# One attention-values product per head, by blocks of keys, in place of two query halves in two slots

## The reference

```
for i in range(S // Q_BLOCK):                       # 4 blocks of 128 queries
    lo, hi = i * Q_BLOCK, (i + 1) * Q_BLOCK
    s = einsum('bhqd,bhkd->bhqk', q[lo:hi], k[:hi]) * scale + cum[lo:hi] - cum[:hi]
    s = where(kpos <= qpos, s, -1e30)
    prob = softmax(s)
    outs.append(einsum('bhqk,bhkd->bhqd', prob, v[:, :, :hi]))   # values
```

## Time and profile before

| | us |
|---|---|
| median of 3 runs (lowest to highest) | 1625.31 (1624.86 to 1625.37) |
| the profiled execution | 1624.74 |
| its span | 1623.0 |
| PE busy in the span | 1604.3 |
| DVE busy | 1027.8 |
| ACT busy | 696.0 |

### The profile page before, as it was taken

The page is one execution under the profiler, slowest core; times in us unless marked ns, Lnnn a source line. Parts: engine busy times, 40 slices in busy tenths (PEclk is TensorE's granted clock), DMA queues, the critical chain, the costliest instruction groups (busy, mean ns, idle before and its releaser), DMA issues.

```text
span 1623.0 us, 19202 instructions
## 1 busy us (share of the span) xinstructions
PE 1604.3 (99%) x7616; PEld 1326.4 (82%) x7616; DVE 1027.8 (63%) x1455; ACT 696.0 (43%) x1016; POOL 174.4 (11%) x255
## 2 busy tenths in 40 slices
PE   9999999999999999999999999999999999999998
PEld 7878777888888888887788887888888888888888
DVE  6755788668384865657744578445567636736757
ACT  6524475545252524414662155342344314414544
POOL 0001145100000000024500255000000000000000
PEclk9999999999999999999999999999999999999999
DMA  5223231265757532331122211323322222222331
GB/s 189 81 89 138 87 128 53 77 209 130 234 130 233 130 104 88 121 130 54 51 104 78 100 56 53 137 97 104 104 91 104 104 92 90 104 104 83 120 109 52
DMA packets 30584, 176.17 MB, mean 109 GB/s; under 512 B 4064, under 2 KB 6560, under 8 KB 11040
## 3 DMA queue, kind: packets, MB, share of 16 engines
q1 hardware_dynamic: 24048, 151.81, 26.0%
q0 software_dynamic: 1728, 12.58, 4.0%
q10 hardware_dynamic: 4720, 10.56, 1.8%
HBM read 170.72 MB, written 4.23 MB: 108 GB/s over the span
## 4 chain that ended last, share of the span: by engine, by line
PE 89%; DVE 5%; issue 2%; ACT 2%; POOL 1%; DMA 1%; SPq 0%; DVEq 0%; POOLq 0%
PE bank L719 22%; PE bank L721 21%; PE bank L720 21%; PE bank L727 3%; PE bank L729 3%; PE bank L728 3%; PE bank L1107 2%; PE bank L1108 2%; PE bank L1109 2%; PE bank L920 1%; PE bank L905 1%; PE bank L1025 1%; DMA x<-in_x_t 1%; DVE q_blk L1991 0%; DVE k_blk L1991 0%
## 5 line engine op out<-in xcount | busy, mean ns | idle before, releaser
L719 PE MATMUL bank<-a_hi,w_hi 128*128 128x512 f32 x1184 | 465.5, 393 | 1.6 <-DVE w_lo L2073 0.9
L721 PE MATMUL bank<-a_hi,w_lo 128*128 128x512 f32 x1184 | 461.2, 390 | 0.0
L720 PE MATMUL bank<-a_lo,w_hi 128*128 128x512 f32 x1184 | 460.9, 389 | 0.0
L1291 ACT ACTIVATE w_hi<-w_raw 128x2048 fp32r<-128x2048 f32 x105 | 200.3, 1908 | 219.0 <-DMA w_raw<-in_strips 215.6
L1854 DVE TENSOR_TENSOR w_lo<-w_raw,w_hi 128x2048 fp32r<-128x2048 f32 x102 | 233.7, 2292 | 48.0 <-ACT w_hi L1291 47.9
L719 PEld LDWEIGHTS bank<-a_hi,w_hi 128*128 128x128 f32 x1184 | 222.4, 188 | 47.5 <-issue 1.4
L721 PEld LDWEIGHTS bank<-a_hi,w_lo 128*128 128x128 f32 x1184 | 222.2, 188 | 46.9
L720 PEld LDWEIGHTS bank<-a_lo,w_hi 128*128 128x128 f32 x1184 | 222.4, 188 | 44.0 <-issue 0.2
L719 PE MATMUL bank<-b_hi,w_hi 128*128 128x512 f32 x368 | 143.4, 390 | 0.4 <-DVE b_lo L2570 0.4
L720 PE MATMUL bank<-b_lo,w_hi 128*128 128x512 f32 x368 | 143.2, 389 | 0.0
L721 PE MATMUL bank<-b_hi,w_lo 128*128 128x512 f32 x368 | 143.2, 389 | 0.0
(11 more groups left out here) (362 smaller groups left out, 2570.3 us busy)
## 6 DMA issues: line engine op xcount, KB each, us to landing
w_raw<-in_strips SPq DMA_DIRECT2D x117, 1024.0 KB, 4.8
a_part<-in_parts SPq DMA_DIRECT2D x15, 1024.0 KB, 7.0
a_part<-in_parts POOLq DMA_DIRECT2D x12, 1024.0 KB, 9.9
seg_in<-cum_kept ACTq DMA_DIRECT2D x16, 256.0 KB, 3.5
spare<-in_parts SPq DMA_DIRECT2D x3, 1024.0 KB, 14.7
spare<-in_strips SPq DMA_DIRECT2D x3, 1024.0 KB, 4.7
x<-in_x_t SPq DMA_DIRECT2D x4, 512.0 KB, 6.8
head_bias<-in_rel ACTq DMA_DIRECT2D x1, 2048.0 KB, 10.5
```

The costliest lines, as they stand in the source:

```text
L719: mm(ps[:, :], w_hi[slot][:, k, cols], hi[:, k, :], start=(k == 0), stop=False)
L720: mm(ps[:, :], w_hi[slot][:, k, cols], lo[:, k, :], start=False, stop=False)
L721: return mm(ps[:, :], w_lo[slot][:, k, cols], hi[:, k, :], start=False, stop=(k == kt - 1))
L1291: run(w_hi[j], w_raw[j], ACT.Copy).then_inc(hi_split, 1)
```

## The change

All values of a head are computed at one place, slot m = 4 head + 7. There they stand ahead of the slot's dense pieces, behind scores(n), where values(head, 1) stood behind turn(n - 2). They go by blocks of keys: for key block 0 one matmul pair (pt_hi, pt_lo) over all four query blocks, for key block 1 a pair over query block 1 and a pair over blocks 2 and 3, for key block 2 a pair over blocks 2 and 3, for key block 3 a pair over block 3. pv_done counts once a head instead of twice, and every wait on it is rewritten: the keep of a head's tiles waits for all values of the head before, where the keep of its tiles 0 and 1 waited for the first half alone.

```diff
+KEY_BLOCKS = [(0, 0, 4, 0), (1, 8, 9, 1), (1, 4, 6, 2), (2, 6, 8, 2), (3, 9, 10, 3)]
...
-                    sp_eng.wait_ge(pv_done, 2 * 3 * HEADS8)
+                    sp_eng.wait_ge(pv_done, 3 * HEADS8)
...
-                def values(head, second):
-
-                    pe.wait_ge(p_lo_done, t0 + TT * head + 2 * second + 2)
-                    if head >= 2 and not second:
+                def values(head):
+
+                    pe.wait_ge(p_lo_done, t0 + TT * (head + 1))
+                    if head >= 2:
                         pe.wait_ge(att_out, h0 + head - 1)
-                    for j in range(2 * second + 2):
-                        alone = j == 2 * second + 1
-                        blocks = BLOCKS[2 * second + 1]
-                        at = range(10)[blocks][j]
-                        cols = slice(at, at + 1) if alone else slice(at - 1, at + 1)
-                        dst = bank[6 + head % 2][:, 256 * second + P * alone:256 * second + 256]
+                    for j, first, end, i in KEY_BLOCKS:
+                        dst = bank[6 + head % 2][:, i * P:(i + end - first) * P]
                         for part in (pt_hi, pt_lo):
...
                 for n in range(SLOTS[call]):
                     if n < TILES and n and (lead is None or n >= 2):
                         scores(n)
+                    if n - late >= 7 and (n - late) % TT == 3:
+                        values((n - late - 7) // TT)
                     for p in slot_pieces(n, call):
                         dense(p)
...
                         turn(n - late - 2)
-                    if n - late >= 5 and (n - late) % 4 == 1 and n - late < TILES + 4:
-                        values((n - late - 5) // TT, 0)
-                    if n - late >= 7 and (n - late) % 4 == 3:
-                        values((n - late - 7) // TT, 1)
...
-                        act.wait_ge(pv_done, 2 * (h0 + head - 1) + i // 2 + 1)
+                        act.wait_ge(pv_done, h0 + head)
...
-                    act.wait_ge(pv_done, 2 * (h0 + head + 1))
+                    act.wait_ge(pv_done, h0 + head + 1)
```

More of the change, by code:

```diff
@@ L906, in turn @@
                     last.then_inc(turned, 1)
-                def values(head, second):
-                    pe.wait_ge(p_lo_done, t0 + TT * head + 2 * second + 2)
-                    if head >= 2 and not second:
+                def values(head):
+                    pe.wait_ge(p_lo_done, t0 + TT * (head + 1))
+                    if head >= 2:
                         pe.wait_ge(att_out, h0 + head - 1)
-                    for j in range(2 * second + 2):
-                        alone = j == 2 * second + 1
-                        blocks = BLOCKS[2 * second + 1]
-                        at = range(10)[blocks][j]
-                        cols = slice(at, at + 1) if alone else slice(at - 1, at + 1)
-                        dst = bank[6 + head % 2][:, 256 * second + P * alone:256 * second + 256]
+                    for j, first, end, i in KEY_BLOCKS:
+                        dst = bank[6 + head % 2][:, i * P:(i + end - first) * P]
                         for part in (pt_hi, pt_lo):
                             last = mm(dst, vs[:, j, head, :, :].rearrange("p s f -> p (s f)"),
-                                      part[:, cols, :].rearrange("p b q -> p (b q)"), start=(j == 0 and part is pt_hi),
+                                      part[:, first:end, :].rearrange("p b q -> p (b q)"), start=(j == 0 and part is pt_hi),
                                       stop=(j > 0 or part is pt_lo), skip_group_check=(j > 0))
```

## The result

| | before | changed |
|---|---|---|
| median us (lowest to highest, 5 runs each) | 1624.95 (1624.86 to 1625.37) | 1650.62 (1645.61 to 1652.04) |
| the profiled execution, its span | 1624.74, 1623.0 | 1645.61, 1643.9 |

The ratio of the times is 1.015, 95% interval 1.0138 to 1.0161. The change makes the kernel slower by some 26 us. The forecast was 1642, the range 1629 to 1652. The profiled execution of the changed kernel is its fastest; the other four are slower than it by up to 6.4 us, where the five of the kernel before lie within 0.5. So there are two questions: where the 20.9 us between the two traces come from, and where the rest comes from.

What follows compares the result with a forecast made beforehand. A once-per-head loop through PE, DVE and ACT was taken to bound the attention calls. 13.6 us for 2a and 2b plus 3.1 for call 1 gave 16.7 more, 1642; own range 1631 to 1650, 8-in-10 range 1629 to 1652.

Steps and rivals of the forecast that it cites:

- E: In each attention head, the end of DVE's low part of the head's last tile, for which PE waits.
- The loop E, PE, scores, DVE and ACT, next E: Once per head in the attention calls: matmuls put between E and the next scores lengthen it; PE's part was 1.56 us.
- Fewer matmuls: Values of each head: 10 matmuls for 12, 1.45 us becoming 1.36, at most 2.2 us of PE's work over 24 heads.
- the 0.96: Us by which scores in a 2a or 2b head were forecast to end later after E: E + 2.52 against E + 1.56.
- The values stand ahead of the dense piece: At the values' new place PE waits 2.06 us for E, and the scores end 0.96 us later.
- The keep of the next head's first tile: ACT's keep waits for all values; the wait grows some 0.5 us but adds nothing beyond the scores' delay.
- The rival of whole waits: PE's extra waits come through whole, 1.5 x 21 heads, 31.5 us more, 1657; chance 0.07.
- the tails: Behind head 6 of 2a and 2b, with no scores left, PE is the bound: 1.5 us later per call.
- The end of call 1: Last values ahead of three dense pieces, so the next product's 0.7 us wait for its fourth operand tile goes away.
- The clock: Rival: idle times of about 2 us per head halve the clock in one stretch, 70 us more, 1712; chance 0.02.

Runs made afterwards that it cites:

- e2: The kernel before with only the second half of the values moved ahead of the slot's dense pieces, still two halves; 1636.98 us, ratio 1.0073.
- e4: The kernel before with the second half of the values one slot later, behind the next scores; 1623.15 us, ratio 0.9987.
- e8: The changed kernel with an extra pv_done count behind key block 0's pair, for which the keep of a head's first tile waits; 1647.97 us, ratio 1.014.
- e1: Against the kernel before, all values of a head in one run, but behind the slot's transposes where the second half stood; 1642.28 us, ratio 1.0108.
- a0_again: The changed kernel run once more, unaltered, for its scatter; 1650.85 us (1647.30 to 1651.43), ratio 1.0153 against the kernel before.
- e9: The kernel with all values in one run behind the transposes, plus an early pv_done count behind key block 0's pair; 1633.60 us, ratio 1.005.
- e6: The changed kernel with four matmuls that compute nothing ahead of the values' wait in all heads; 1649.76 us.
- e7: The changed kernel with four matmuls that compute nothing ahead of the values' wait, only in heads 0 to 6 of 2a and 2b; 1647.12 us, ratio 1.0138.

## Why the prediction was right, and where not

*What bounds the kernel.* The loop E, PE, scores, DVE and ACT, next E is shown: E-to-scores grew by 1.12 us in the head of the timeline and the loop by 1.12; the stretch behind the scores kept its length; e2 put 0.7 into it and e4 took the values out, with the signs the loop gives.

*Fewer matmuls.* 1.36 us for the ten were forecast. Where PE doesn't wait they take 1.34, as PE's timeline of the changed kernel in call 1 shows:

```profile
249.79 0.40 PE L918 MATMUL bank<-pt_hi,vs 128*128 128x512 f32 x1
250.03 0.40 PE L918 MATMUL bank<-pt_lo,vs 128*128 128x512 f32 x1
...
251.13 0.45 PE L721 MATMUL bank<-y_hi,w_hi 128*128 128x512 f32 x1
```

In the head above they take 1.43 (1012.68 - 1011.25), since the first one behind a wait steps 0.34 (1011.59 - 1011.25) for 0.24 here (250.03 - 249.79). Only two of the 24 heads have the 1.34; the others have 1.42 to 1.45, and before the two halves of nearly every head took 0.49 and 0.96, 1.45 together. So the waiting takes back nearly all that the merging was to give. Together with the dense piece behind the values (0.75 for 0.69, its first matmul stepping 0.29 for 0.23) this is most of the 0.16 by which the 1.12 exceeds the 0.96.

*The values stand ahead of the dense piece.* Right: e2 alone gives +11.7. The wait at the values is 1.48 us in the head where I had 2.06, and only 0.87 or 0.88 in eight of the twelve loops of 2a and 2b, for 1.5 to 2 forecast: PE reaches the values later than I had put it. The length of the loop doesn't hang on that, since PE waits for E either way.

*The keep of the next head's first tile.* This is the step that was wrong in part. "Lies inside the delay already counted" holds in the middle heads of the changed kernel (e8 leaves their loops at 9.2 us). It fails in the first heads of 2a and 2b; in that of 2a DVE has a weight split behind that low part. DVE there, in the changed kernel (E = 766.60), and below it the split and the maximum in the kernel before (E = 762.05):

```profile
768.67 0.29 DVE L2009 TENSOR_TENSOR pt_lo_2a<-bank,pt_hi_2a 128x128 fp32r<-128x128 f32 x1 [1.63 <-ACT pt_hi_2a L1347]
768.88 1.52 DVE L1865 TENSOR_TENSOR w_lo<-w_raw,w_hi 128x1024 fp32r<-128x1024 f32 x1
770.33 0.41 DVE L1999 CUSTOM_DVE_ANT_0 score_2a<-bank,future 128x256 f32<-128x256 f32 x1
...
762.70 1.25 DVE L1869 TENSOR_TENSOR w_lo<-w_raw,w_hi 128x1024 fp32r<-128x1024 f32 x1
763.86 0.41 DVE L2003 CUSTOM_DVE_ANT_0 score_2a<-bank,future 128x256 f32<-128x256 f32 x1
```

The maximum comes at E + 3.73 (in the first head of 2b at E + 3.41), not at the E + 2.9 of the other heads: 1.63 us of idling, and then 1.5 us of work that before ran while PE was on its way to the scores. The rival of whole waits had named this as its condition, that PE delays the others twice in a head. Outside the new place the semaphore is no detail: it is 8.7 of the 17.0 us of e1.

*Sizes.* Between the traces, from the first scores of call 1 to those of 2a 4.6 us were added (forecast 3.1), from there to those of 2b 8.5 (6.8), and in the rest 7.8 (6.8): 20.9 for 16.7. The six loops of 2a are 6.7 us longer together and those of 2b 5.7, for 5.3 forecast, single ones between 0.65 and 1.83; the tails, from head 6's E to head 7's, are 1.4 and 1.7 longer, for 1.5. In call 1 the sum hides luck: six loops at 0.47 were forecast, and they grew by 0.26, 0.01, 0.01, 0.81, 0.03 and 1.42, which is 2.5 for 2.8. The lower end of the forecast's own range was mis-added as well: 1625.3 and half of the delay, 8 us, is 1633 and not 1631.

*The end of call 1.* Wrong sign: the wait for b_lo grew from 0.7 to 1.4 us. No run tried it, but the traces show the path. DVE before, then ACT and DVE now:

```profile
307.64 0.69 DVE L2223 TENSOR_TENSOR x<-x,bank 128x512 f32<-128x512 f32 x1 [3.19 <-PE bank L721]
309.14 0.69 DVE L2019 TENSOR_TENSOR qk<-qk,bank 64x512 f32<-64x512 f32 x1 [0.21 <-ACT qk L1356]
...
310.24 0.59 ACT L1352 ACTIVATE qk<-bank 64x512 f32<-64x512 f32 x1 [2.83 <-PE bank L918]
312.38 0.69 DVE L2219 TENSOR_TENSOR x<-x,bank 128x512 f32<-128x512 f32 x1 [4.25 <-PE bank L723]
313.69 0.69 DVE L2015 TENSOR_TENSOR qk<-qk,bank 64x512 f32<-64x512 f32 x1
```

The values stand ahead of the dense pieces now, and ACT's copy is done before these end. But DVE's add (line 2015) stands behind the evacuation of the dense unit (line 2219) in its order, and that waits for those pieces. So the rows are no earlier against the dense work, and PE no longer has the last eight values matmuls (0.88 us, 307.44 to 308.32) between the dense pieces and the product that waits for b_lo. The step that failed is "the output rows are ready earlier": it looked at PE's order and not at DVE's.

*The clock.* A rival with a chance of 0.02 and a price of 70 us. Its mechanism came true and its price did not: the falls last 3.4 to 6.8 us, not a whole call, and cost up to 6 us an execution; 7 of the 10 executions have mean clocks of 0.994 to 0.996. They explain 5 of the 8.6 us between forecast and median, so the sum is to be held against the 1645.6 at the full clock, not against the median. The section "HAM oscillation — how this bites in real kernels" of the Trainium skill, page "TensorE: Matmul & The Clock Gate", tells of a kernel whose waits between bursts of matmuls brought the clock down in every round. This case's trace agrees in part: a0_again has three falls behind single waits of 0.2 to 1.1 us, but they come in three heads only, and in the first profile in none.

*The sum of the parts.* Place (11.7) and merging with early release (8.5) make 20.2, the merged semaphore in the changed place 1.5 by the loops of e8, together 21.7, for the 20.9 between the two traces without a fall. The clock adds its 5 to that in the median. The agreement is no closer than an us or two: the profile of e9 holds a fall too, so its 8.5 may hold some of the clock, and that the parts simply add is assumed. The parts can't be told apart further from these runs.

## What to carry to other kernels

An engine that is 99% busy can still be part of a loop with others; find the event that it waits for once per round, and ask of every move whether it puts work between that event and the instruction that the others wait for. Fusing two pieces of work fuses their semaphores too: count who was released by the first half, and what stands behind that waiter in its engine's order. Work that has nothing to do with the loop belongs ahead of the wait as cover, and what the others wait for belongs first behind it.

## What the runs showed of the hardware

The granted clock fell to 1.2 GHz for 3.4 or 6.8 us at a time in a program in which PE is 98% busy over the whole span (a0_again), each time after three waits of 0.2 to 1.1 us in close sequence, and in some executions of the same program and not in others. With matmuls that compute nothing in the waits, no fall shows in the two profiles (e6, e7), and the kernel was 3.7 us faster (e7). And a 512-column matmul right behind a wait steps 0.33 to 0.34 us to its successor in 22 heads of the changed kernel, where it steps 0.24 in the two heads in which nothing was waited for: the waiting itself costs 0.1 us beyond its length.
